# A two-layer streaming encoder step: three edits to the order of VectorE's and GpSimd's work

## The reference

```python
def _swiglu(x, w_in, w_out):
    gate, up = jnp.split(x @ w_in, 2, axis=-1)
    return (jax.nn.silu(gate) * up) @ w_out

def _trunk(x, p, cache, w):
    for li in range(DEPTH):                     # 2
        hn = _rmsnorm(h, w['norm_mix_g'][li])
        ...                                     # layer 0: RG-LRU and windowed attention; layer 1: mLSTM
        h = h + y
        h = h + _swiglu(_rmsnorm(h, w['norm_ffn_g'][li]), w['ffn_w_in'][li], w['ffn_w_out'][li])
        h = h + jax.nn.sigmoid(h @ w['ple_w_gate'][li]) * (p[li] @ w['ple_w_proj'][li])
    y_out = _rmsnorm(h, w['final_g'])
```

## Time and profile before

| | us |
|---|---|
| median of 3 runs | 2952.69 (2950.7 to 2953.35) |
| the profiled execution, its own time | 2951.0 |
| its span from first to last instruction | 2949.2 |
| PE busy | 2759.7 (94%) |
| DVE busy | 1543.8 (52%) |
| POOL busy | 945.5 (32%) |
| ACT busy | 600.8 (20%) |
| mean granted TensorE clock | 0.974 of full speed |

### The profile page before, as it was taken

The page is one execution under the profiler, slowest core; times in us unless marked ns, Lnnn a source line. Parts: engine busy times, 40 slices in busy tenths (PEclk is TensorE's granted clock), DMA queues, the critical chain, the costliest instruction groups (busy, mean ns, idle before and its releaser), DMA issues.

```text
span 2949.2 us, 40946 instructions
## 1 busy us (share of the span) xinstructions
PE 2759.7 (94%) x17240; PEld 2695.2 (91%) x17240; DVE 1543.8 (52%) x2332; ACT 600.8 (20%) x1266; POOL 945.5 (32%) x439
## 2 busy tenths in 40 slices
PE   7899989999999999998999989799999999999996
PEld 6798889999999999998999977699999999999996
DVE  7856474444444444667664056446444444444565
ACT  3434331000000000134122155322000000000032
POOL 3322053333333333333433310023333333333430
PEclk9898999999999999999999999899999999999998
DMA  3101111111111111113122221311111111111111
GB/s 132 40 22 59 45 58 37 43 44 43 44 42 45 43 40 48 49 45 111 46 68 88 90 76 52 137 37 50 44 43 44 43 43 44 43 44 43 46 42 59
DMA packets 57831, 160.10 MB, mean 54 GB/s; under 512 B 7341, under 2 KB 28333, under 8 KB 56369
## 3 DMA queue, kind: packets, MB, share of 16 engines
q1 hardware_dynamic: 31056, 109.79, 12.0%
q10 hardware_dynamic: 26592, 47.70, 4.5%
HBM read 137.07 MB, written 20.40 MB: 53 GB/s over the span
## 4 chain that ended last, share of the span: by engine, by line
PE 81%; DVE 11%; issue 4%; ACT 3%; POOL 0%; ACTq 0%; DMA 0%; DVEq 0%; POOLq 0%
PE ps L413 25%; PE ps L415 25%; PE ps L414 25%; DVE hl L1019 3%; DVE tmpb L1013 2%; PE ps L816 1%; PE ps L586 1%; PE ps L853 1%; PE ps L616 1%; DVE xl L904 1%; DVE uc L1175 1%; DVE hb L1480 1%; PE ps L598 0%; DVE cs L1454 0%; DVE rstd L897 0%
## 5 line engine op out<-in xcount | busy, mean ns | idle before, releaser
L413 PE MATMUL ps<-xh,wh 128*128 128x352 f32 x3432 | 1123.1, 327 | 35.7 <-DVE xl L904 21.9
L414 PE MATMUL ps<-xl,wh 128*128 128x352 f32 x3432 | 1115.0, 325 | 0.0
L415 PE MATMUL ps<-xh,wl 128*128 128x352 f32 x3432 | 1114.8, 325 | 0.0
L461 POOL TENSOR_TENSOR wh<-raw,seeds 128x1024 fp32r<-128x1024 f32 x208 | 419.5, 2017 | 1918.8 <-PE ps L415 1912.3
L413 PEld LDWEIGHTS ps<-xh,wh 128*128 128x128 f32 x3432 | 652.3, 190 | 41.2 <-issue 27.7
L414 PEld LDWEIGHTS ps<-xl,wh 128*128 128x128 f32 x3432 | 652.0, 190 | 2.1 <-issue 0.4
L415 PEld LDWEIGHTS ps<-xh,wl 128*128 128x128 f32 x3432 | 652.0, 190 | 0.0
L463 POOL TENSOR_TENSOR wl<-raw,wh 128x1024 fp32r<-128x1024 f32 x208 | 528.1, 2539 | 16.3
L1006 DVE TENSOR_TENSOR tmpa<-ps,rstd 128x352 f32<-128x352 f32 x132 | 69.1, 524 | 717.4 <-PE ps L415 717.4
L413 PE MATMUL ps<-hh,wh 128*128 128x352 f32 x1056 | 351.4, 333 | 60.6 <-DVE x L1044 60.6
L414 PE MATMUL ps<-hl,wh 128*128 128x352 f32 x1056 | 348.8, 330 | 0.0
(11 more groups left out here) (263 smaller groups left out, 2513.5 us busy)
## 6 DMA issues: line engine op xcount, KB each, us to landing
raw<-wstream SPq DMA_DIRECT2D x208, 512.0 KB, 3.6
vod<-stage ACTq DMA_DIRECT2D x72, 128.0 KB, 1.9
vb<-vod ACTq DMA_DIRECT2D x9, 512.0 KB, 4.0
ob<-vod ACTq DMA_DIRECT2D x9, 512.0 KB, 3.7
x<-xT ACTq DMA_DIRECT2D x3, 1408.0 KB, 12.6
x<-xT ACTq DMA_DIRECT2D x2, 2112.0 KB, 8.3
xsave<-x ACTq DMA_DIRECT2D x1, 4224.0 KB, 11.5
x<-xsave ACTq DMA_DIRECT2D x1, 4224.0 KB, 14.4
```

Of the source, the lines that this page charges most:

```text
L413: pe.matmul(out, whi, mhi, start=first, stop=False)
L414: pe.matmul(out, whi, mlo, start=False, stop=False)
L415: return pe.matmul(out, wlo, mhi, start=False, stop=last)
L461: pool.tensor_tensor(hi, raw[:, r, :], zero, ALU.add).then_inc(hi_made, 1)
```

## The change

Three edits, and one small shift that goes with the first:

- **Additions before the last lows.** In an FFN, `hidden` no longer ends with product 5, low 4 and low 5. For all chunks but the first they are handed to `add`, which does two additions, product 5, four additions, low 4, four additions, low 5, and the other 14 additions.
- **Constants behind the first convolution.** `log1p` and what follows it moves from DVE's start to the place behind `conv(0)` and units 9 to 11. ACT waits for `sp_ready` only behind the first six sigmoids. `norm_sum` comes behind units 3, 6 and 9 rather than 2, 6 and 9.
- **Blocks 3 and 4 wait.** POOL splits an FFN's third block (and so its fourth, and all later ones) only when all 24 lows of the FFN's input are made. POOL's nested loop is written as a single one to say this; its other waits are as before.

```diff
+            later = {B0_FFN + 2: "ffn0", B1_FFN + 2: "ffn1"}
+            for b in range(NBLK):
+                j, r = b % NW, b % NRAW
+                pool.wait_ge(raw_landed[r], 16 * (b // NRAW + 1))
+                pool.wait_ge(block_done, b + 1)
+                if b in later:
+                    pool.wait_ge(xl_ready, 1 + XLN[later[b]] + KT * NT)
...
-                if u in (2, 6, 9):
-                    norm_sum(0, (2, 6, 9).index(u))
+                if u in (3, 6, 9):
+                    norm_sum(0, (3, 6, 9).index(u))
...
                         if v >= 1:
-                            product(v - 1)
+                            product(cx, v - 1)
                         if v >= 2:
-                            low(v - 2)
-                    product(5)
-                    low(4)
-                    low(5)
-
-                def add(cx, b):
+                            hidden_low(cx, par, v - 2)
+
+                def add(cx, b, rest=None):
                     for u in range(24):
                         mo, tt = u // 3, u % 3
+                        if rest is not None and u == 2:
+                            product(rest, 5)
+                        if rest is not None and u in (6, 10):
+                            hidden_low(rest, (rest - c0) % 2, 4 + (u - 6) // 4)
...
                 hidden(c0, b0, 0)
+                product(c0, 5)
+                hidden_low(c0, 0, 4)
+                hidden_low(c0, 0, 5)
...
-                        add(c0 + 2 * i + j, b0 + 4 + 12 * i + 6 * j + 4)
+                        add(c0 + 2 * i + j, b0 + 4 + 12 * i + 6 * j + 4, c0 + 1 + 2 * i + j)
...
-            dve.wait_ge(lam_exp, 1)
-            log1p(z_, e_, q_, p_)
...
             conv(0)
             outs(9, 10, 11)
+            dve.wait_ge(lam_exp, 1)
+            log1p(z_, e_, q_, p_)
...
+            gates(0)
             act.wait_ge(sp_ready, 2)
-            gates(0)
```

More of the change, by code:

```diff
@@ L452, in _ @@
             pool.wait_ge(zero_ready, 1)
[L453 to L463, removed]
+            later = {B0_FFN + 2: "ffn0", B1_FFN + 2: "ffn1"}
[5 more added lines that the diff above has]
+                    pool.wait_ge(xl_ready, 1 + XLN[later[b]] + KT * NT)
+                hi = wh[:, j, :, :].rearrange("p k c -> p (k c)")
+                lo = wl[:, j, :, :].rearrange("p k c -> p (k c)")
+                pool.tensor_tensor(hi, raw[:, r, :], zero, ALU.add).then_inc(hi_made, 1)
+                pool.wait_ge(hi_made, b + 1)
+                pool.tensor_tensor(lo, raw[:, r, :], hi.bitcast(F32), ALU.subtract).then_inc(raw_free, 1)
         def split_count(b):
@@ L994, in ffn, with product, hidden_low @@
                 c0 = FCH * layer
+                def product(cx, v):
+                    dve.wait_ge(pair_read, 6 * cx + v + 1)
+                    dve.wait_ge(sil_ready, 6 * cx + v + 1)
+                    dve.tensor_tensor(tmpb[:, v % 3, :], tmpb[:, v % 3, :], tmpa[:, v % 3, :],
+                                      ALU.mult).then_inc(h32_ready, 1)
+                def hidden_low(cx, par, v):
+                    f, tt = v // 3, v % 3
+                    dve.wait_ge(hh_ready, 6 * cx + v + 1)
+                    dve.tensor_tensor(hl[:, par, f, tt * TW:(tt + 1) * TW], tmpb[:, v % 3, :],
+                                      hh[:, par, f, tt * TW:(tt + 1) * TW].bitcast(F32),
+                                      ALU.subtract).then_inc(hl_ready, 1)
                 def hidden(cx, b, par):
@@ L1008, in scale @@
                                           ALU.mult).then_inc(pair_read, 1)
[L1010 to L1021, removed]
                     for v in range(6):
@@ L1186, in _ @@
             outs(9, 10, 11)
+            dve.wait_ge(lam_exp, 1)
+            log1p(z_, e_, q_, p_)
+            step(dve.tensor_scalar(mx, lam, -1.0, 0.0, ALU.mult, ALU.max))
+            step(dve.scalar_tensor_tensor(mx, p_, 2.0, mx, ALU.mult, ALU.add))
+            dve.tensor_scalar(sp4, mx, 4.0, None, ALU.mult).then_inc(sp_ready, 1)
+            dve.tensor_scalar(sp8, mx, -8.0, None, ALU.mult).then_inc(sp_ready, 1)
             for t in range(AT):
```

## The result

The changed kernel takes **2845.36 us** (median of 4 runs, 2844.14 to 2848.94), the kernel before in runs beside it 2952.52 (4 runs, 2950.7 to 2953.35). The ratio is 0.964, with a 95% interval of 0.9623 to 0.9657: 107.2 us less. Direction and mechanisms held; two sizes did not, that of a wait of PE and that of the constants.

A forecast was written before the change was run, and what follows sets the result against it. PE was taken to bound the kernel, busy 94% of the span, with gains only from its idle and low-clock time. 81.0 + 11.6 + 4.0 = 96.6 us off 2951.0 made 2854.4, forecast 2856 by the median; range 2848 to 2877.

The forecast's parts named there:

- Part 1: FFN chunks, additions before the last lows: PE's 20 stalls and the slow stretches behind them go, 81.0 us.
- Rival (d): The FFN stall moves whole to unit 10 or the next up's first pair, leaving parts 2 and 3: 2937; chance 0.04.
- (a): POOL keeps DVE out for both instructions of a split; unit 10 late in each chunk, up to 20 us back, 2876; chance 0.08.
- So all 60.6 us go: At down's unit 8, PE's idle time waiting for DVE's additions, 60.6 us in 20 pieces, vanishes entirely.
- The bound of 92: Upper bound for the moved additions' gain in us: 60.6 + 20 x 1.57, if all 20 stalls had a slow stretch.
- the slow stretches: Low-clock time of PE behind 13 of 20 FFN stalls, 1.57 us each, should go too: 20.4 us.
- Rival (b): In the FFNs slow stretches come without the stalls, so only 60.6 of the 81.0 us come: 2876; chance 0.07.
- Rival (c): Slower than before: the clock falls by itself under the FFNs' steady PE work, over 61 falls undoing everything; chance 0.02.
- The forecast's share of 0.39: Loss in an FFN slow stretch as a share of its length, read from 11 to 18 matmul starts.
- Part 2: The two turns into an FFN, blocks 3 and 4 held back: 6.7 + 2.5 + 2.4 = 11.6 us, bounds 5 and 14.
- Part 3: The start, constants moved behind the first convolution so lows begin earlier: 4 us, bounds 2 and 7.
- the last three come singly behind POOL's instructions, the eighth at about 23.3: At the start, the first strip's last three lows each wait for a POOL split; the unit ends at 24.2.

The follow-up runs named there:

- e8: The changed kernel with product 5 of a chunk ahead of its first addition instead of behind the second: 2850.17 us.
- e9: The changed kernel with product 5 and low 4 ahead of the first addition, low 5 still behind the tenth: 2914.97 us.
- after: The changed kernel itself, with all edits, in its first profile: 2845.36 us.
- e3_hold: The kernel before with only the holding back of an FFN's blocks 3 and 4: 2941.17 us.
- e5: The kernel before with only ACT's wait for the constants moved behind the first six sigmoids: 2951.21 us.
- e7: The changed kernel with ACT's wait for the constants put back ahead of the first six sigmoids: 2849.22 us.
- e1: The kernel before with only the additions moved before the last lows: 2865.63 us.
- after_again: The changed kernel run and profiled once more, beside later variants on one chip: 2845.22 us.
- e2: The kernel before with only the constants moved behind the first convolution, with ACT's new order and the later norm sum: 2943.5 us.
- e4: The changed kernel with layer 1's second weight block split only when the 24 lows of the mixer's input are made: 2839.54 us.
- e4_again: The same kernel as e4, run again beside the changed kernel on one chip: 2836.15 us.
- e11: e4 with, in addition, the third block of the start split only when the first strip's 8 lows are made: 2834.09 us.

## Why the prediction was right in kind and short in size

**Part 1, the stall goes whole: right.** No row of PE waits for line 1050, DVE's timeline is the one worked out, to 0.1 us up to product 5. Rival (d), the stall moves whole, is out. So is (a): product 5 ended in the middle of POOL's pair, in the changed kernel (659.39, POOL's second instruction runs until 661.74) as before. e8 shows how near it was: 2.1 us later on DVE, and PE just begins to feel it, while e9's 4.7 us later bring 2.59 us of idle time back. The 2.2 us to spare that the forecast counted were real. Additions do go on beside POOL, as forecast: four in 1.80 us at 659.39.

**Part 1, its size: the first term was mis-sized.** "So all 60.6 us go" took a wait at its idle time. It costs 0.27 us more, 0.16 of them because the row counts idle time from the listed end of the matmul before, and 0.11 in a longer first step: 3.30 against 3.03 in the kernel before, 2.86 against 2.59 in e9, 0.27 against nothing shown in e8. Twenty times 0.27 is 5.4 us, half of what the forecast was short. It was to be had from the rows of before: the period of 72.85 less 3.03 gave 69.8, and it was compared with nothing. Down's own 24 units of 0.96 came to 23.0; from down's first start to the next up's it was 26.30. So part 1 was worth 86.4 us where the sum had 81.0. The bound of 92 had the same fault, but it was not what placed the range: its low end took the upper bounds of parts 2 and 3 and left part 1 at 81 (81 + 14 + 7 = 102 us, 2849). With part 1's own bound it would have been 92 + 14 + 7 = 113 us, 2840 by the median, and the result would have lain inside.

**Part 1, the slow stretches: right.** 13 in 20 were forecast from six in nine of the first FFN; 7 and 6 were there, and the trace of after has none. (They could have been counted in the trace of before, which holds all 20; that six in nine carried over so well is luck.) Rival (b) is refuted by 1050 us at a clock of 1.00, and by e9, in which they return with the stalls, nine in 20. Rival (c), which made the kernel slower, is refuted by the same rows: PE runs without a pause at the 2.4 GHz level for 650 us.

On the clock the Trainium skill ("TensorE: Matmul & The Clock Gate", on the oscillation in real kernels) counts a penalty of half the throttled time. The forecast's share of 0.39 was a misreading: the 11 and 18 of the earlier trace rows count the matmuls that were running at some time in the stretch, not those started. The steps give it: 0.293 us in the slow stretch and 0.160 outside, a loss of 1 - 0.160/0.293 = 0.45. So this trace nearly agrees with the page; the sum, which went by the 1.57 us, was not touched by it.

**Part 2: right in kind, size between.** 1.43 us of idle time at FFN 0 for the 1.6 forecast, none at layer 1's norm sum. The whole profile gives 6.54 and 5.13 us up to the two FFNs, and the low clock behind the first pair (2.8 us at 0.50, 1.27 us lost) falls inside FFN 0: 12.9 us for the 11.6 forecast; e3_hold alone gave 9.7. At the fourth pair nothing waited: POOL had its blocks ready at 435.9, and PE wanted them at 444.4 in the changed kernel.

**Part 3: the size was wrong, 4 for 7 to 9.** Three terms failed, all on the low side. First, "the last three come singly behind POOL's instructions, the eighth at about 23.3": six lows were done by 15.9 and only two came behind POOL, the eighth at 20.65. PE's last low step shows it:

```profile
20.71 0.42 PE L413 MATMUL ps<-xh,wh 128*128 128x352 f32 x1 [1.59 <-DVE xl L907]
```

The unit ended at 21.3 instead of 24.2; before it had ended at 29.84, so 8.5 us were gained there and 8.7 by the first convolution. I had counted a low too many behind POOL; the gap of POOL's wait for its load took four, not three. Second, in this execution no 1.3 us were lost to the low clock: it was at its full level from 18.3 us on, before the eighth low, so the work behind ran at the high level. In others that loss did come, as said below. Third, ACT's order had been given no price. It takes 1.28 us of table load out of the way (e5's rows), and the stretch from the convolution to the first product, 17.9 us before, is 17.3 now; with the old order on ACT and the moved constants it is 21.3 (e7). That the log1p is hidden was right; no row speaks against the norm sum's shift at nothing.

**The parts together.** Of the 10.2 us of span by which the forecast was short, part 1 has 5.4, part 2 1.3 and part 3 5.35, less the 1.9 lost behind FFN 0.

**The spread at the start.** With the small instructions first, the convolution started at 70.4 to 70.5 in every profile (before, e1, e3, e5); without, at 60.1 to 65.5 (after, after_again, e2, e4, e4_again, e7 to e11). The profile of the changed kernel had 61.79, a better one than the mean of some 63; so of the 9.35 us some 1 to 2 are that execution's. Two things in the traces go with this spread. The first is how many lows fall behind POOL's instructions: the eighth ends at 16.89 with POOL held back (e11) and at 18.42 to 22.33 without. The second is the clock. In after and after_again the eighth low ends at the same time, 20.65 and 20.59, but the stretch behind it reads, first in after, then in after_again:

```profile
21.30:24.50 3.20, 3.20 (x21) 3.20 (x21) 3.09 (x2) 0.50 (x1) 3.12 (x2) 1.00 0.49 157
21.30:24.50 3.20, 3.20 (x13) 3.20 (x12) 3.09 (x2) 0.74 (x1) 3.12 (x2) 0.50 0.46 166
```

The convolution starts at 61.79 in the first and at 63.27 in the second, 1.5 us later. So the 1.3 us that the forecast set aside for the low clock are lost in some executions of this kernel and not in others.

**What stays open.** What decides whether the clock falls is not shown, neither at the start nor behind a stall nor in the mixer of layer 1. The shift of the norm sum was not tried alone.

## What to carry to other kernels

Take the cost of a wait on PE from the time between two equal points of the loop with and without it, not from the idle time that the row shows. In this kernel a wait took 0.27 us more than its row shows, and a stall of 3 us was followed by a slow stretch of 1.57 us in 13 of 20 cases: the 20 stalls were worth 86.4 us for 60.6 of idle time. Where two engines disturb one another, order the one that is waited for so that what PE needs stands ahead of what merely has to be done, and hold the disturbing work back where PE does not yet need it: the same hold, at layer 1's gates and at the start, gave a further 11 us.

## What the runs showed of the hardware that was not expected

- A wait of PE costs about 0.27 us over the idle time shown (3.30 for 3.03 before, 2.86 for 2.59 in e9), and a delay too short to leave idle time shows as two long steps (0.32 and 0.27 us instead of 0.16 each, e8).
- PE kept the 2.4 GHz level through 650 us without a pause. Stalls of 3.03 us were followed by a slow stretch in 13 of 20 cases, those of 2.59 us in 9 of 20, delays without idle time (e8's FFNs) in none.
- DVE's additions that read PSUM went on at 0.44 us each beside POOL's splits, while a product or a low, with all operands in SBUF, that met a split ended only behind POOL's instruction: 1.01 to 2.72 us in the rows for what takes 0.50. DVE got in between the two instructions of a block each time that it stood waiting there, in 73 of the changed kernel's 208 blocks, and ended 0.38 us behind the first; POOL's second instruction was then 2.53 to 2.58 us long, where with none of these DVE instructions beside it it was 2.34 to 2.42.
- A table load of ACT (1.28 us) ran ahead of the wait of the first activation that needs it (67.30 in e5), and behind a wait written before that activation (80.91 in the kernel before). Two lines exchanged moved it from the path into idle time (e5, e7).
